# Second layer: one weight split ahead of the first statistic, variance sums read later; end of the program rearranged

## The reference

```python
h = modulate(rmsnorm(x, g_mix[l]), sh1, sc1)              # context tokens: the same with their own shifts
q, k, v, u = split_in(h @ w_in[l])                         # 8 query heads, 2 key/value heads, conv input u
q, k = rope_2d(q), rope_2d(k)
a_out = latent_attention(q, k, v, k_ctx, v_ctx, sink)      # window of +-128 tokens, plus all context keys
z = u[..., :512] * sigmoid(u[..., 512:])
cv_out = silu(layernorm(depthwise_conv31(z) + b_dw, ln_g, ln_b))
x = x + gt1 * concat(rmsnorm(a_out, g_a), rmsnorm(cv_out, g_c)) @ w_out
x = x + gt2 * swiglu(modulate(rmsnorm(x, g_ffn), sh2, sc2))
return rmsnorm(x, g_final)                                 # after the second layer, latent tokens only
```

## Time and profile before

| what | us |
|---|---|
| median of 3 runs (1589.21 to 1590.46) | 1590.11 |
| the profiled execution, its own time | 1588.25 |
| its span | 1586.4 |
| TensorE busy (97% of the span; 86% of the chain that ended last) | 1533.7 |
| VectorE busy (59%) | 936.5 |
| ScalarE busy (34%) | 536.9 |
| GpSimd busy (8%) | 128.4 |
| mean granted TensorE clock, of full speed | 0.991 |

### The profile page before, as it was taken

The page is one execution under the profiler, slowest core; times in us unless marked ns, Lnnn a source line. Parts: engine busy times, 40 slices in busy tenths (PEclk is TensorE's granted clock), DMA queues, the critical chain, the costliest instruction groups (busy, mean ns, idle before and its releaser), DMA issues.

```text
span 1586.4 us, 24584 instructions
## 1 busy us (share of the span) xinstructions
PE 1533.7 (97%) x9714; PEld 1274.5 (80%) x9714; DVE 936.5 (59%) x1571; ACT 536.9 (34%) x858; POOL 128.4 (8%) x163
## 2 busy tenths in 40 slices
PE   6999998999999999999999999998999999999996
PEld 3865764688888888888888888676679998998995
DVE  2584689767666325765654466678786443443445
ACT  3312378724222112221122243148844222322222
POOL 0033221040000000000000001511020000000000
PEclk9999999999999999999999999999999999999998
DMA  9582600012333223333522123410022332323222
GB/s 358 207 242 58 241 12 27 1 54 107 119 122 103 67 81 144 119 115 123 191 74 62 54 70 108 137 54 1 28 67 93 93 93 93 93 93 95 93 87 83
DMA packets 39865, 161.16 MB, mean 102 GB/s; under 512 B 5616, under 2 KB 6000, under 8 KB 33648
## 3 DMA queue, kind: packets, MB, share of 16 engines
q1 hardware_dynamic: 35856, 148.72, 27.6%
q0 software_dynamic: 3936, 11.45, 2.6%
HBM read 149.76 MB, written 2.10 MB: 96 GB/s over the span
## 4 chain that ended last, share of the span: by engine, by line
PE 86%; DVE 6%; ACT 4%; issue 2%; POOL 1%; DMA 1%; SPq 0%; DVEq 0%; ACTq 0%; POOLq 0%
PE banks L496 74%; PE banks L525 3%; PE banks L613 2%; PE banks L433 1%; PE banks L640 1%; PE banks L625 1%; POOL z_padded L1528 1%; DVE row_max L1132 1%; PE banks L677 1%; PE banks L465 1%; ACT prob L819 1%; PE banks L483 1%; ACT w_high L736 1%; DMA ada_first<-in_w_ada 1%; ACT probT L831 1%
## 5 line engine op out<-in xcount | busy, mean ns | idle before, releaser
L496 PE MATMUL banks<-h_high,w_high 128*128 128x512 f32 (+1 forms) x1856 | 433.0, 314 | 3.9 <-DVE w_low L1015 2.4
L496 PE MATMUL banks<-h_high,w_low 128*128 128x512 f32 (+1 forms) x1856 | 427.8, 312 | 0.0
L496 PE MATMUL banks<-h_low,w_high 128*128 128x512 f32 (+1 forms) x1856 | 426.5, 311 | 0.0
L736 ACT ACTIVATE w_high<-raw 128x1024 fp32r<-128x1024 f32 (+1 forms) x178 | 185.3, 1041 | 697.0 <-PE banks L496 677.7
L496 PEld LDWEIGHTS banks<-h_high,w_high 128*128 128x128 f32 x1856 | 288.0, 189 | 38.3 <-issue 14.6
L1015 DVE TENSOR_TENSOR w_low<-raw,w_high 128x1024 fp32r<-128x1024 f32 (+1 forms) x178 | 216.3, 1215 | 171.1 <-ACT w_high L736 167.5
L496 PEld LDWEIGHTS banks<-h_low,w_high 128*128 128x128 f32 x1856 | 287.7, 189 | 21.1
L496 PEld LDWEIGHTS banks<-h_high,w_low 128*128 128x128 f32 x1856 | 286.4, 189 | 20.6
L1059 DVE COPY shift_product<-banks 128x2 f32<-128x2 f32 x116 | 18.4, 159 | 310.1 <-PE banks L496 299.2
L496 PE MATMUL banks<-ff_high,w_high 128*128 128x512 f32 (+1 forms) x528 | 160.5, 358 | 0.6 <-DVE ff_low L1389 0.6
L496 PE MATMUL banks<-ff_high,w_low 128*128 128x512 f32 (+1 forms) x528 | 159.6, 357 | 0.0
(11 more groups left out here) (171 smaller groups left out, 1623.5 us busy)
## 6 DMA issues: line engine op xcount, KB each, us to landing
raw<-in_w_gu SPq DMA_DIRECT2D x88, 512.0 KB, 3.5
ada_raw<-in_w_ada SPq DMA_DIRECT2D x21, 1024.0 KB, 5.7
raw<-in_w_dn SPq DMA_DIRECT2D x32, 512.0 KB, 3.5
raw<-in_w_mix SPq DMA_DIRECT2D x28, 512.0 KB, 5.0
ada_in_ff<-in_w_ada SPq DMA_DIRECT2D x12, 1024.0 KB, 5.5
raw<-in_w_out SPq DMA_DIRECT2D x16, 512.0 KB, 3.5
ada_first<-in_w_ada SPq DMA_DIRECT2D x7, 1024.0 KB, 14.1
raw<-in_w_dn SPq DMA_DIRECT2D x16, 384.0 KB, 3.0
```

What stands on the lines that cost most here:

```text
L496: last = mm(bank[:, 2 * slot + bk, 0:b - a], weights[w][:, k0_w + k, :], rhs[:, k0_rhs + k, a:b], start=(k == 0 and n == 0), stop=(k == kt ...
L736: f(wH[j][:, 0:k, :], raw[j][:, 0:k, :], ACT.Copy).then_inc(w_high, 1)
```

## The change

In the second layer ScalarE makes the high part of the third weight block of `u` before the first norm's root and its copy, and VectorE the low part before the diagonals. In the second layer's value block TensorE reads the variance sums behind k-tile 3 instead of 0 and makes the broadcast behind k-tile 7 instead of 5. At the end, ScalarE computes a root of one column ahead of the last down phase, so that the table load stands there; it multiplies tiles 0 and 1 by the final gain; TensorE makes five unread products before the last sums and four behind them, and makes the last broadcast a second time into the next bank; ScalarE copies that one to `inv_root`, and GpSimd multiplies tiles 0 and 1 by it. VectorE makes the other six. The outputs of tiles 0 and 1 stand fourth and eighth in SyncE's order.

```diff
+        BY_POOL = (0, 1)
@@ sync
-            for k in range(DT):
-                sp.wait_ge(y_ok, k + 1)
+            for n, k in enumerate(k for k in range(DT) if k not in BY_POOL):
+                sp.wait_ge(y_ok, n + 1)
                 sp.dma_start(out[k], x[:, k, 0:N]).then_inc(y_out, 16)
+                if n % 3 == 2:
+                    sp.wait_ge(y_pool, n // 3 + 1)
+                    sp.dma_start(out[BY_POOL[n // 3]], x[:, BY_POOL[n // 3], 0:N]).then_inc(y_out, 16)
@@ tensor
-                                   [(0, lambda: stat_tokens((layer, "var"), blocks)),
-                                    (5, lambda: stat_broadcast((layer, "var"), blocks))] if 2 * i + j == V_TILE else ())
+                                   [(3 * layer, lambda: stat_tokens((layer, "var"), blocks)),
+                                    (5 + 2 * layer, lambda: stat_broadcast((layer, "var"), blocks))]
+                                   if 2 * i + j == V_TILE else ())
...
+            keep_busy(5)
             stat_tokens((DEPTH, "n1"), NB)
+            keep_busy(4)
             stat_broadcast((DEPTH, "n1"), NB)
+            mm(bank[:, BC + 1, 0:N], ones[:], scratch[:, 0:N], start=True, stop=True).then_inc(bc_again, 1)
@@ scalar
                 if layer:
+                    split_high(layer, "u", 0, 0)
                     root((layer, "n1"), TB)
                     copy_root((layer, "n1"), T)
...
                 for i in range(PAIRS_OF["u"]):
-                    split_high(layer, "u", i, 0)
+                    if layer == 0 or i:
+                        split_high(layer, "u", i, 0)
...
+                    if c == 2 and layer + 1 == DEPTH:
+                        f(esink[:, 0:1], eps[:], ACT.Sqrt)
...
+            for k in BY_POOL:
+                f(x[:, k, 0:N], x[:, k, 0:N], ACT.Copy, scale=col("g_final", k)).then_inc(g_ok, 1)
             root((DEPTH, "n1"), NB)
+            act.wait_ge(bc_again, 1)
+            f(rs[:, 0:N], bank[:, BC + 1, 0:N], ACT.Copy).then_inc(rs_ok, 1)
@@ vector
                 if layer:
+                    split_low(layer, "u", 0, 0)
                     diagonal((layer, "n1"), TB)
...
-                    split_low(layer, "u", i, 0)
+                    if layer == 0 or i:
+                        split_low(layer, "u", i, 0)
...
-            for k in range(DT):
+            for k in (k for k in range(DT) if k not in BY_POOL):
                 stt(out=x[:, k, 0:N], in0=x[:, k, 0:N], scalar=col("g_final", k), in1=wide[:, 512 * BC:512 * BC + N],
@@ gpsimd
+            pool.wait_ge(rs_ok, rs_index[DEPTH, "n1"] + 1)
+            for n, k in enumerate(BY_POOL):
+                pool.wait_ge(g_ok, n + 1)
+                nc.gpsimd.tensor_tensor(x[:, k, 0:N], x[:, k, 0:N], rs[:, 0:N], ALU.mult).then_inc(y_pool, 1)
```

More of the change, by code:

```diff
@@ L264, in hybrid_backbone @@
         ff_high, ff_low = sem("ff_high_ready"), sem("ff_low_ready")
-        y_ok = sem("out_tile_ready")
+        y_ok, y_pool = sem("out_tile_ready"), sem("out_tile_ready_by_pool")
+        g_ok, bc_again = sem("out_tile_gained"), sem("final_root_broadcast_again")
         dve_self, pool_self = sem("dve_self"), sem("pool_self")
@@ L670, in attention @@
                     values(len(qs) - 1, m)
-            pe.wait_ge(consts, 5)
-            pe.wait_ge(cond_ok, 1)
             def keep_busy(n):
@@ L677, in keep_busy @@
                     mm(bank[:, 3, 0:2 * P], ones[:], cond[:].rearrange("p k v -> p (k v)"), start=True, stop=True)
+            pe.wait_ge(consts, 5)
+            pe.wait_ge(cond_ok, 1)
             for k in range(DT):
```

## The result

The changed kernel is slightly slower: 1590.9 us (median of 20 runs, 1589.3 to 1595.0) against 1588.55 (20 runs of the kernel before beside them, 1586.1 to 1594.4), a ratio of 1.0015 with a 95% interval of 1.0009 to 1.0022. That lies within the 0.2% that the prediction calls no change, so its likeliest case was the right one. The direction wasn't: a gain of 2.6 us was forecast and the interval lies wholly on the slower side. The range (1584.6 to 1590.2) missed too: 1587.5 was forecast, 3.4 us less than measured. In the profiled executions the span grew from 1586.4 to 1588.9, though the mean granted clock rose from 0.991 to 0.995.

What follows compares the result with a forecast made beforehand. TensorE, nearly always busy, was taken as the bound, with costly waits and clock falls behind them. Terms -2.8 + 1.6 - 1.4 = -2.6 us took the median of 1590.11 to 1587.5 us, range 1584.6 to 1590.2.

Steps and rivals of the forecast that it cites:

- likeliest case: Whole kernel: time the same as before, within about 0.2% (3.2 us), chance 0.54; faster had 0.42, slower 0.04.
- Part A: Second layer's start: earlier weight split shortens TensorE's wait by 1.4 us and restores its clock for 1.4, together -2.8 us.
- the clock fell only behind the waits of over 2 us: Second layer's third block: with 1.0 us idle instead of 2.4, full clock expected, worth 1.4 us (bounds 0 and 1.6).
- Part B: Second layer's value block: later sums, GpSimd starts earlier and VectorE's rotary work stands still, +1.6 us (bounds -0.9 and +2.9).
- TensorE's new idleness in the last query block costs nothing: Attention's entry: free if the second score product is there before the second exponential at 1080.9; no cost counted.
- Part C: Program's end: dummies keep the clock up, so VectorE's last products start 1.4 us earlier, -1.4 us (bounds -2.4 and +2.0).
- Rival 3: Program's end: clock low at the small products, dummies last 3.5 us, end +2.0, sum +0.8, 1590.9 us; chance 0.12.
- the two products on GpSimd bring 0 to 0.1: Program's end: outputs follow the first tile at DMA pace, so moving two products to GpSimd gains 0 to 0.1 us.

Runs made afterwards that it cites:

- b_only: Kernel before with only the second layer's variance sums moved behind k-tile 3 and the broadcast behind k-tile 7: 1589.04 us, ratio 0.9998.
- gpsimd_only: Kernel before with two last products on GpSimd, their gains on ScalarE, second broadcast and output order; no dummies or early table: 1594.18 us, ratio 1.0027.
- all_but_gpsimd: Changed kernel without its GpSimd part, VectorE making all eight last products: 1587.14 us, ratio 0.9986 to the kernel before.
- a_and_c: Changed kernel without GpSimd's products, variance sums and broadcast back at k-tiles 0 and 5: 1584.48 us, 0.9975 of before; on another chip 1585.43 us, 0.9976.
- silus_first: Kernel of all_but_gpsimd with ScalarE's two copies of query 3 behind the four silus in the second layer: 1583.9 us, ratio 0.9972 to the kernel before.
- a_only: Kernel before with only the weight split moved ahead of the second layer's first statistic: 1585.56 us, ratio 0.9975.
- products_behind_rotary: Kernel of all_but_gpsimd with GpSimd waiting in the second layer for query 3's rotary result before its four products: 1585.46 us, 0.9979 of before.

## Why the prediction was wrong

**Part A, -2.8: right.** The third block started 1.1 us behind its forerunner instead of 2.4 and at full clock, and the first split of `qkv` came 2.75 us earlier. The runs part this into its two terms: the shorter wait gives 1.3 (1.4 forecast), and the clock alone 1.4, for in b_only, with the wait of 2.40 but at full clock, the same split came 1.43 earlier than in the kernel before. So the clock's share was right as a size. As a rule ("the clock fell only behind the waits of over 2 us") it fails both ways: b_only and gpsimd_only kept the full clock behind the same 2.40 us, and the clock did fall behind shorter waits, in the kernel before to 0.52 (1095.5 to 1098.5) behind 1.84 us in attention, in the changed kernel behind the 1.55 us shown above.

**Part B, +1.6: right mechanism, undersized.** The new wait of the broadcast (1.7 forecast, 1.66 measured), the three rotary durations (1.3 to 2.1 forecast, 1.42 to 1.77) and the exponential's delay of 1.6 came as played through. The step that failed is "TensorE's new idleness in the last query block costs nothing ... played at half clock it is there at 1080.0 to 1081". I counted the score product at half clock, but not the transposes of the values behind it, nor the copy that waits for them. This term is +2.6 by the end of attention; the missed 1.0 is TensorE's at half speed.

**Part C: VectorE and the outputs right, the end wrong.** The clock stayed at 1.00, VectorE started 1.25 us earlier (1.4 forecast), the outputs ran at a DMA share of 1.02 and 382 GB/s. SyncE waited 0.4 us for one of GpSimd's tiles (0.1 forecast), and from VectorE's first last product to SyncE's end it is 7.8 us against 7.7 before, so the two tiles gained nothing. Rival 3 gave 1590.9 us, which is what was measured, but its mechanism (a low clock under the dummies) isn't there: the number fits by accident. The failed step, and the one that decides the whole, is "the two products on GpSimd bring 0 to 0.1". I looked at whom they serve and not at what ends the program. The bound from below was 0 because the trace of before seemed to show nothing that they delay. It did: GpSimd's last instruction there ends at 1179.8, and the drain behind it at 1188.3, one row of 10.66 us in the view by line of L127, 400 us away from anything that waits. Moving GpSimd's last work to the end uncovers **4.3 us** of it, which outweighs the whole forecast of -2.6.

**The rest.** The median of before used as the base was 1590.11; the kernel before beside the changed one gave 1588.55. By that base the forecast would have been 1586.0, and the miss 4.9 instead of 3.4: the base's luck hid a part of the error. The terms as the traces show them, -0.4 - 2.8 + 2.6 - 1.3 + 4.3, account for the spans within 0.1.

**What stays open.** On many runs the parts don't add up as they do in the traces: A alone -4.0, C -2.4, but both together -4.0 and -3.8; B alone 0, but 1.7 beside A (all_but_gpsimd less a_and_c; 2.7 by their medians and in the traces). With intervals of 1.5 us either way the first is no contradiction. The second agrees with the two traces: beside A, B cost 1.6 by the rotary work and 1.1 by the clock (2.7 by the end of attention); alone 1.6 by the rotary work, none by the clock at attention, and 1.4 were won back by the clock behind the split. Whether the other executions were like these isn't known. The kernel before varies in this place too: in gpsimd_only's execution, where B's code is that of before, the wait for GpSimd's sum was as long (3.2 us), but the half-speed stretch behind it took 3.6 us instead of 6.9. Before (windows, columns as in rows 2):

```profile
1061.00:1065.00 4.00, 4.00 (x14) 3.43 (x14) 2.38 (x7) 2.69 (x4) 0.00 (x0) 0.51 0.13 12
```

and in gpsimd_only:

```profile
1058.00:1061.40 3.40, 3.40 (x12) 2.92 (x12) 1.62 (x5) 2.46 (x4) 0.00 (x0) 0.50 0.01 2
1061.50:1065.00 3.50, 3.50 (x21) 3.07 (x20) 3.07 (x8) 1.31 (x2) 0.00 (x0) 1.00 0.37 68
```

So the broadcast came earlier, GpSimd started earlier relative to the rotary work, and two of the three rotary instructions stood still as well (timeline):

```profile
1066.24 0.75 DVE L1229 SCALAR_TENSOR_TENSOR diagonals<-diagonals,shift_product_rotated,sinT 128x512 f32<-128x512 f32 x1
...
1066.53 6.26 POOL L1539 TENSOR_TENSOR z_padded<-z_padded,sq 128x512 f32<-128x512 f32 x4 [9.61 <-ACT sq L764]
1066.91 1.79 DVE L1230 SCALAR_TENSOR_TENSOR tmp<-tmp,shift_product,cosT 128x512 f32<-128x512 f32 x1
...
1068.73 1.67 DVE L1232 TENSOR_TENSOR tmp<-tmp,diagonals 128x512 f32<-128x512 f32 x1
```

There attention ended at +190.4, 0.8 us later than in the profiled execution of before. How often that happens isn't known from one profile a kernel. Nor is it settled why the clock falls behind one idle time of 2.40 us and not behind another, or why it stays low longer in one execution.

**The better version** is a_and_c, 0.9975 and 0.9976 on two chips with the shortest span of all (1581.9, twice): it leaves out the two parts that cost. By the ratios it can't be told from silus_first (0.9972 [0.9959, 0.9984]), from a_only (0.9975 [0.9965, 0.9985]) or from products_behind_rotary (0.9979 [0.9970, 0.9988]), and that part C adds to part A is seen in the traces only. All four intervals lie below the kernel before, and further below the changed one.

## What to carry to other kernels

Before work is given to an engine that had long been done, look at what its end of program costs and what hides it: list each engine's last row, and ask of every part of a change not only whom it serves but what it makes last. When an earlier start is bought, check which engine then runs beside it: two instructions that hold each other up can eat the gain, and an added wait can give it back. Listing each engine's end of program found the term that the sum had left out, and running each part alone confirmed it.

## What the runs showed of the hardware

- GpSimd's drain at the end of the program ends 8.4 us behind its last instruction, whatever that was: 8.37 and 8.41 behind two products, 8.43 behind a memset of 0.10 us, 8.46 behind an addition that ended at 1180 us. VectorE's and TensorE's end with their work (1580.4 and 1577.1 in the changed kernel). In none of the runs did the program end before GpSimd's drain. The row of the wait (L127 for "PEq") names the wrong engine.
- A VectorE instruction with two SBUF inputs takes 1.42 to 1.79 us instead of 0.69 to 0.75 where it meets GpSimd's products. GpSimd's four took 6.3 us where they met the rotary work, and 5.9 and 6.1 in products_behind_rotary and before, where they met less of VectorE.
- Idle times of equal length (2.40 us, same place) were followed by a granted clock of 0.54 in the execution of before and 1.00 in those of b_only and gpsimd_only, which moved what comes behind by 1.4 us. Behind equal waits of 3.2 us at another place the clock stayed low for 6.9 us in one execution and 3.6 in another.
